# The per-layer products of a hybrid decoder layer, moved from the first expert block into the first attention tile

## The chip, the cores and the metric

The kernel runs on one core of a Trainium2 chip, in float32. The metric is the device time of one execution in microseconds (us). TensorE (PE) multiplies, VectorE (DVE) and ScalarE (ACT) work on elements, GpSimd (POOL) does small operations and indexed transfers, and SyncE (SP) issues most of the DMA transfers. Each engine takes its own instructions strictly in order; they meet only at semaphores.

## The reference

One layer: attention with two groups of heads, a mixture of experts, and a gated embedding per layer (PLE), at SEQ = 512 and D = 1024.

```python
a = rms_norm(h, g_mix); proj = a @ w_in
h = h + concat([o_moba, o_gla]) @ w_out          # two groups of heads
f = rms_norm(h, g_ffn)
h = h + moe_ffn(f, w_router, b_router, w1, b1, w2, b2)   # top 4 of 32 experts
ple = rms_norm(p @ w_ple_proj, g_ple)            # p (512, 256), w_ple_proj (256, 1024)
h = h + sigmoid(h @ w_ple_gate) * ple
return rms_norm(h, g_final)
```

The products `p @ w_ple_proj` depend on inputs alone. They are wanted only at the very end.

## The kernel before

The order of the work on each engine is written out by hand, and semaphores with counts tie the engines together. The stages are: projections (group by group, until 161 us); attention in four tiles of 128 queries, `t` = 0 to 3, each with steps `j` = 0 to 5 on PE (scores, softmax on DVE and ACT, transposed probabilities, values); routing; a first expert block (block 0), written out apart from the rest; a loop over the other blocks of 96 rows; and the tail.

While PE works on attention tile t, it multiplies the mixed heads of tile t - 1 with w_out (`mix_out`, line 1023), DVE adds the halves to H (`add_mix`), and ACT squares the row (`h_square`, line 745). From the square come the mean, the power on POOL, the normed row for the experts (line 1459), and the logits. For the last tile the same chain leads on to the row table `row_of` (line 1650), from which POOL gathers the rows of block 0 (`gather`), PE transposes them, and ACT and DVE take them apart in a high half `XTh` and a low half `XTl`.

Every matrix of the experts is multiplied as a sum of two halves of reduced width. A weight chunk (1 MB, 128x2048) is loaded by SP (`load_chunk`, line 411) into one of six slots, its high half is made by ACT (`split_hi`, line 782) and its low half by DVE (`split_lo`, line 1531), in a ring HL of four. `w_lo` counts the low halves done. Block 0 takes the chunks in the order 0, 1, 2, 3, 8, 6, 7, 9, 10, 11. Slots 0 to 3 lie in the large buffer W, slots 4 and 5 (`W45`) where `wst[:, 0]` lies, the staging buffer of w_in and of the first half of w_out. The bias b1 goes to `b1raw`, ACT copies its high half to BB ahead of `XTh` (line 796), and DVE makes its low half (line 1665) ahead of `XTl`.

The PLE work stood in block 0. SP loaded w_ple_proj and p into `wst[:, 0]` when w_out was nearly done with (lines 461 and 462). PE transposed p (line 1151, to `pT`) and made 16 products of 128x128 by 128x512 in float32 (`ple_tile`, line 1180), each of which the trace shows as two pieces. ACT squared each tile of results straight from PSUM (line 804), POOL took the power, and ACT scaled it (line 808) into `pleo`, in `wst[:, 1]`.

## Time and profile before

| | |
|---|---|
| median of 3 runs | 1537.45 us (1536.6 to 1537.8) |
| the profiled execution | 1536.28 us |
| its span, first to last instruction | 1534.1 us |
| mean granted TensorE clock | 0.988 of 2.4 GHz |
| start of attention, entry into the loop of experts | 162 us, 361.6 us |
| PE busy, DVE busy, ACT busy | 97%, 83%, 65% |

All places in the trace are given in us from the span's start. A row of the timeline reads: start, length, engine, line, operation, output and inputs, count, and in brackets how long the engine had been idle and who released it. Pieces that are merged into one row follow each other without a gap worth mention. A row of the chain reads start, length, what. A busy share says nothing of which engine is late; the chain and the brackets do.

### The profile page before, as it was taken

To read this page: it belongs to the slowest core of one execution; us is meant where nothing else is said; L and a number is where in the kernel's file an instruction comes from. 1 tells how busy PE (TensorE), PEld (TensorE's weight loads), DVE (VectorE), ACT (ScalarE), POOL (GpSimd) and SP (SyncE) were. 2 spreads that over 40 slices of the span, in tenths; PEclk is the share of its full clock that TensorE was granted. 3 is DMA by queue.
4 is the path that set the end of the run, shared out by engine and by line. 5 is a ranking of instruction groups with operands and counts; after the bars stand their busy time and mean duration, and the time that the engine had idled before them with its cause. 6 is when DMAs were issued, how large, how long until landed. Compare 5 with 4: busy or idle time off the path is not lost.

```text
span 1534.1 us, 20725 instructions
## 1 busy us (share of the span) xinstructions
PE 1494.5 (97%) x7115; PEld 1041.7 (68%) x7115; DVE 1280.0 (83%) x1109; ACT 1004.8 (65%) x919; POOL 198.5 (13%) x148
## 2 busy tenths in 40 slices
PE   7999899999999999999999999999999999999997
PEld 5878555566666666676666666666666666666666
DVE  5322356689999999999999999999999999999974
ACT  5432333457777777777777777777777777777642
POOL 6000000020211111111111121111111111111000
PEclk9999799989999999999999999999999999999999
DMA  5215400459999999999999999999999999999921
GB/s 171 98 67 192 178 15 14 157 188 355 374 393 370 372 376 381 375 379 381 380 382 376 377 377 370 375 372 387 373 384 376 382 381 375 380 376 367 380 100 55
DMA packets 126384, 466.58 MB, mean 304 GB/s; under 512 B 7955, under 2 KB 8518, under 8 KB 126358
## 3 DMA queue, kind: packets, MB, share of 16 engines
q1 hardware_dynamic: 118432, 438.73, 75.5%
q0 software_dynamic: 7312, 25.40, 6.8%
q10 hardware_dynamic: 614, 2.11, 0.3%
q8 instruction: 16, 0.26, 0.1%
q14 instruction: 10, 0.08, 0.0%
HBM read 446.67 MB, written 19.53 MB: 304 GB/s over the span
## 4 chain that ended last, share of the span: by engine, by line
PE 94%; DVE 2%; issue 2%; ACT 2%; DMA 0%; POOL 0%; DVEq 0%; POOLq 0%; ACTq 0%
PE ps L1217 46%; PE ps L1249 23%; PE ps L1004 9%; PE ps L1023 3%; PE ps L1347 2%; PE ps L1205 1%; PE ps L1256 1%; PE ps L1232 1%; PE ps L1180 1%; PE ps L1082 1%; PE ps L1070 1%; PE ps L1098 1%; PE ps L1108 1%; PE ps L1042 0%; DMA b_all<-in_b_router_dram 0%
## 5 line engine op out<-in xcount | busy, mean ns | idle before, releaser
L1531 DVE TENSOR_TENSOR HL<-W,HL 128x2048 fp32r<-128x2048 f32 x384 | 881.7, 2321 | 43.2 <-ACT HL L782 40.5
L782 ACT ACTIVATE HL<-W 128x2048 fp32r<-128x2048 f32 x382 | 731.9, 1917 | 174.7 <-PE ps L1217 100.6
L1217 PE MATMUL ps<-HL,XTh 128*96 128x512 f32 x2048 | 563.5, 397 | 0.5 <-DVE XTl L1527 0.5
L1217 PEld LDWEIGHTS ps<-HL,XTh 128*96 128x96 f32 x2048 | 323.2, 162 | 132.9 <-issue 1.9
L1217 PE MATMUL ps<-HL,XTl 128*96 128x512 f32 x1024 | 319.7, 393 | 0.0
L1249 PE MATMUL ps<-HL,HIDTh 128*96 128x512 f32 x1024 | 280.9, 396 | 1.7 <-DVE HIDTl L1559 1.3
L1249 PEld LDWEIGHTS ps<-HL,HIDTh 128*96 128x96 f32 x1024 | 162.7, 161 | 81.8 <-issue 13.2
L1217 PEld LDWEIGHTS ps<-HL,XTl 128*96 128x96 f32 x1024 | 165.2, 161 | 70.5
L600 POOL DMA_INDIRECT y_sums<-actT,row_of x31 | 60.8, 1962 | 949.4 <-ACT actT L841 949.4
L1249 PE MATMUL ps<-HL,HIDTl 128*96 128x512 f32 x512 | 159.6, 393 | 0.0
L1249 PEld LDWEIGHTS ps<-HL,HIDTl 128*96 128x96 f32 x512 | 82.7, 161 | 35.3
L1392 DVE TENSOR_TENSOR PWl<-wst,PWh 128x1024 fp32r<-128x1024 f32 x24 | 29.0, 1223 | 69.0 <-ACT PWh L667 68.1
L583 POOL DMA_INDIRECT XG<-f_rows,row_of x33 | 83.6, 2534 | 17.3 <-DVE row_of L1650 8.2
L812 ACT ACTIVATE HIDTh<-ps 128x384 fp32r<-128x384 f32 x64 | 31.5, 492 | 61.3 <-PE ps L1256 61.1
L1023 PE MATMUL ps<-wst,actT 128*128 128x512 f32 x128 | 58.9, 603 | 0.0
L673 ACT ACTIVATE W<-ps 128x512 f32<-128x512 f32 x20 | 11.9, 594 | 65.2 <-PE ps L1004 65.2
L729 ACT ACTIVATE M<-M,nmax 128x128 f32<-128x128 f32 (+3 forms) x32 | 18.0, 561 | 46.3 <-DVE nmax L1500 46.2
L1555 DVE TENSOR_TENSOR HIDr<-T,SIG 96x512 f32<-96x512 f32 x64 | 44.0, 688 | 5.0
L1497 DVE SCALAR_TENSOR_TENSOR M<-dist,ps 128x128 f32<-128x128 f32 (+3 forms) x32 | 15.4, 483 | 36.7 <-PE ps L1070 27.9
L817 ACT ACTIVATE SIG<-T 96x512 f32<-96x512 f32 x64 | 40.0, 624 | 9.3 <-DVE T L1543 8.3
L823 ACT ACTIVATE XTh<-ps 128x768 fp32r<-128x768 f32 x32 | 26.0, 813 | 28.3 <-PE ps L1217 26.0
L1543 DVE TENSOR_SCALAR T<-ps 96x512 f32<-96x512 f32 x64 | 43.5, 679 | 1.0 <-PE ps L1217 1.0
(270 smaller groups left out, 1378.8 us busy)
## 6 DMA issues: line engine op xcount, KB each, us to landing
W<-in_w_dram SPq DMA_DIRECT2D x384, 1024.0 KB, 8.3
wst<-in_w_in_dram SPq DMA_DIRECT2D x6, 2048.0 KB, 8.6
H<-in_x_dram SPq DMA_DIRECT2D x8, 512.0 KB, 5.0
wst<-in_w_out_dram SPq DMA_DIRECT2D x2, 2048.0 KB, 10.9
W<-in_w_ple_gate_dram SPq DMA_DIRECT2D x4, 1024.0 KB, 7.7
y_sums<-M SPq DMA_DIRECT2D x1, 2688.0 KB, 15.5
f_rows<-M ACTq DMA_DIRECT2D x4, 512.0 KB, 2.6
out_dram<-TL SPq DMA_DIRECT2D x4, 512.0 KB, 2.6
```

Of the source, the lines that this page charges most:

```text
L583: pool.indirect_dma_start(XG[:], None, f_rows, bass.IndirectOffsetOnAxis(ap=row_of[:, b:b + 1].bitcast(U32), axis=0)).then_inc(xg_in, 16)
L600: pool.indirect_dma_start(y_sums, bass.IndirectOffsetOnAxis(ap=rows.bitcast(U32), axis=0), YR, None, compute_op=ALU.add).then_inc(y_added, 16)
L782: act.activation(HL[:, k % HRING, 0], w_slot(k), ACT.Copy).then_inc(w_hi, 1)
L812: act.activation(HIDTh[:, 4 * h:4 * h + 4], ps[:, 2 * h, 0:4 * CAP].rearrange("p (f j) -> p f j", f=4), ACT.Copy).then_inc(hth_out, 1)
L817: act.activation(SIG[:], T1[:], ACT.Sigmoid, scale=ALPHA).then_inc(sig_done, 1)
L1004: last = pe.matmul(ps[:, g % 4], l, r, start=(c == 0 and m == 0), stop=(c == NC - 1 and m == 2))
L1023: last = pe.matmul(ps[:, bank], actT[:, c, t * P:(t + 1) * P], wst[:, n, c], start=(c == first_c), stop=(c == last_c))
L1217: last = pe.matmul(ps[0:CAP, 2 * h + n], xt[:, c], HL[:, s, part, cc * 1024 + n * 512:cc * 1024 + (n + 1) * 512], start=(h == 0 and c == 0 ...
L1249: last = pe.matmul(ps[0:CAP, 4 + n], ht[:, f], HL[:, s, part, ff * 1024 + n * 512:ff * 1024 + (n + 1) * 512], start=(f == 0 and ht is HIDT ...
L1531: dve.tensor_tensor(HL[:, k % HRING, 1], w_slot(k if ready is None else k - 4), HL[:, k % HRING, 0].bitcast(F32), ALU.subtract).then_inc(w ...
L1543: dve.tensor_scalar(t1, ps[0:CAP, 2 * h:2 * h + 2, 0:512:2], LIMIT, None, ALU.min).then_inc(glu_min, 1)
L1555: dve.tensor_tensor(HIDr[:, h * 512:(h + 1) * 512], T2[:], SIG[:], ALU.mult).then_inc(hid_ready, 1)
```

## The change

The PLE products go into attention tile 0. PE transposes p at step 0 and makes two halves of a tile at each of the steps 1 to 4 (`ple_half`), into PSUM banks 3 and 2, and ACT copies them out (`ple_out`). ACT squares them in tile 1 and scales them in tile 2, one tile of results at each of the steps 0 to 3; one operation of DVE and one of POOL, at the start of tile 2, serve all four. The results stay in the first 4096 columns of W. Weight slots 0 and 1, which were there, move to `W01`, which lies where `wst[:, 1]` lies, the second half of w_out. Their first chunks are therefore loaded once that half has been used, for which PE now multiplies the last tile's second half first. On DVE the low half of chunk 0 is made later.

```diff
-        wpp = wst[:, 0, 0:4, :]...
-        prow = wst[:, 0, 4:6, :]...
-        pT = wst[:, 0, 6:8, :]
-        pleo = wst[:, 1, :, :]...
+        wpp = in_w(18432, 2, D)
+        prow = in_w(20480, NT, PLE)
+        pT = in_w(21504, 2, SEQ)
+        pleo = in_w(0, NT, D)
...
-            return W[:, s * 2048:(s + 1) * 2048] if s < 4 else W45[:, s - 4]
+            return W01[:, s] if s < 2 else W[:, s * 2048:(s + 1) * 2048] if s < 4 else W45[:, s - 4]
...
                 if n == 0:
                     sp.wait_ge(p_lo, 24)
+                    sp.wait_ge(st_ready, 14)
+                    sp.wait_ge(kt_ready, 2)
+                    sp.dma_start(wpp, w_ple_proj[0]...).then_inc(ple_ld, 16)
+                    sp.dma_start(prow, p[0, 0]...).then_inc(ple_ld, 16)
...
-            for k in range(2):
-                load_chunk(sp, 0, k, 0)
             sp.wait_ge(s_done, NT * MH)
             for k in range(2, 4):
                 load_chunk(sp, 0, k, 0)
             sp.wait_ge(wo_done, 2 * NT - 1)
-            sp.dma_start(wpp, w_ple_proj[0]...).then_inc(ple_ld, 16)
-            sp.dma_start(prow, p[0, 0]...).then_inc(ple_ld, 16)
+            for k in range(2):
+                load_chunk(sp, 0, k, 0)
             sp.wait_ge(w_lo, 1)
             load_chunk(sp, 0, 6, 0)
...
-            sp.wait_ge(pp_done, NT)
             for k in range(10, NK):
                 load_chunk(sp, 0, k, 0)
...
             for t in range(NT):
+                if t == 2:
+                    pool.wait_ge(pp_ms, 1)
+                    pool.tensor_tensor(rstd[:, 0:NT], ss[:, 0:NT], mhalf[:, 0:NT], ALU.pow).then_inc(pp_rs, 1)
                 go_rstd(t)
...
+            def ple_out(j):
+                if j == 0:
+                    for c in range(2):
+                        act.wait_ge(pt2_done, c + 1)
+                        act.activation(pT[:, c], ps[:, 3 - c], ACT.Copy).then_inc(pt2_out, 1)
+                else:
+                    for i in (2 * j - 2, 2 * j - 1):
+                        act.wait_ge(pp_done, i + 1)
+                        act.activation(pleo[:, i // 2, (i % 2) * 512:(i % 2 + 1) * 512], ps[:, 3 - i % 2], ACT.Copy).then_inc(pp_out, 1)
...
+                    if t == 0:
+                        ple_out(j)
                     for i in (2 * j - 2, 2 * j - 1):
                         if j >= 1:
                             pt_copy(t * MH + i)
+                    if t == 1 and j < NT:
+                        ple_square(j)
+                    if t == 2 and j < NT:
+                        ple_scale(j)
...
             split_x(0)
-            ple_square(0)
             choose_bias(0)
-            ple_scale(0)
-            ple_square(1)
             split_hi(0, 8)
-            ple_scale(1)
-            ple_square(2)
-            ple_scale(2)
-            ple_square(3)
-            ple_scale(3)
             split_hi(0, 6)
...
-                first_c, last_c = (4, 3) if last_tile and n == 0 else (0, NC - 1)
-                bank = 5 - n if last_tile else 3
+                first_c, last_c = (4, 3) if last_tile else (0, NC - 1)
+                bank = 4 + n if last_tile else 3
...
+                    if t == 0 and j == 0:
+                        turn_ple()
+                    elif t == 0 and j <= MH // 2:
+                        ple_half(2 * j - 2)
+                        ple_half(2 * j - 1)
...
                     if j == MH // 2:
                         pe.wait_ge(on_ready, t + 1)
+                        if t == 0:
+                            pe.wait_ge(pp_out, 2 * NT)
...
-            split_lo(0, 0)
-            half_turned(T3, 0, 2 * T3 + 1)
-            add_mix(T3, 1, 4)
-            half_turned(T3, 1, 2 * T3 + 2)
+            half_turned(T3, 1, 2 * T3 + 1)
+            add_mix(T3, 0, 4, 2 * T3 + 2)
+            half_turned(T3, 0, 2 * T3 + 2)
...
             dve.wait_ge(x_asked, 1)
+            split_lo(0, 0)
             split_lo(0, 1)
             dve.wait_ge(bb_hi, 1)
```

SP's queue from the attention tiles to the first expert block, before. `in_w` is an expert's weight chunk, `in_b` the bias; the waits are in brackets, by semaphore.

```order
L411 DMA W<-in_w_dram 128x2x1024 x2
L411 DMA W<-in_w_dram 128x2x1024 [waits s_done]
L411 DMA W<-in_w_dram 128x2x1024
L461 DMA wst<-in_w_ple_proj_dram 128x2x1024 [waits wo_done]
L462 DMA wst<-in_p_dram 128x4x256
L411 DMA W<-in_w_dram 128x2x1024 [waits w_lo]
L467 DMA actT<-in_b_dram 32x512 [waits lg_done]
```

And now:

```order
L413 DMA W<-in_w_dram 128x2x1024 [waits s_done]
L413 DMA W<-in_w_dram 128x2x1024
L413 DMA W<-in_w_dram 128x2x1024 [waits wo_done]
L413 DMA W<-in_w_dram 128x2x1024
L413 DMA W<-in_w_dram 128x2x1024 [waits w_lo]
L471 DMA actT<-in_b_dram 32x512 [waits lg_done]
```

Chunks 0 and 1 stood ahead of the wait for the scores and now stand behind the wait for the last tile's w_out products. The wait for `w_lo` stands where it stood, ahead of chunk 6 and the bias.

DVE behind the last tile's ranks, before. The row with HL is the low half of chunk 0, `ps` is PSUM, `ss` the mean of the FFN norm:

```order
L1610 TENSOR_TENSOR M<-it_j,Js 128x1152 [waits dve_step]
L1531 TENSOR_TENSOR HL<-W,HL 128x2048 [waits w_hi]
L1463 COPY actT<-ps 128x4x128 [waits ft_done]
L1449 TENSOR_TENSOR H<-H,ps 128x512 [waits wo_done]
L1463 COPY actT<-ps 128x4x128 [waits ft_done]
L1365 TENSOR_SCALAR ss<-ss 128x1 [waits h_ss]
```

And DVE now, from the row table on, where the low half of chunk 0 has gone:

```order
L1649 SCALAR_TENSOR_TENSOR row_of<-ps,none 96x32 [waits dve_step]
L1654 TENSOR_REDUCE s<-ex 128x4 [waits e_out]
L1655 RECIPROCAL s<-s 128x4 [waits dve_step]
L1656 TENSOR_TENSOR gate<-ex,s 128x16 [waits dve_step]
L1657 TENSOR_SCALAR extra<-cnt 128x32 [waits dve_step]
L1659 SCALAR_TENSOR_TENSOR extra<-cnt,extra 128x32 [waits dve_step] x4
L1660 SCALAR_TENSOR_TENSOR xend<-ones,extra 128x32 [waits dve_step]
L1531 TENSOR_TENSOR HL<-W,HL 128x2048 [waits w_hi,x_asked,dve_step]
L1531 TENSOR_TENSOR HL<-W,HL 128x2048 [waits w_hi]
L1665 TENSOR_TENSOR BB<-actT,BB 128x512 [waits bb_hi]
```

The low half of chunk 0 has moved past both halves of the last tile, the logits, the row table and the request for the gathered rows, and stands directly ahead of that of chunk 1.

ACT at the end of attention, now as before but for the line numbers; the four rows with HL are the high halves of chunks 0 to 3, the row with H the square of the last tile:

```order
L806 ACTIVATE HL<-W 128x2048 [waits w_slot_in0]
L806 ACTIVATE HL<-W 128x2048 [waits w_slot_in1]
L806 ACTIVATE HL<-W 128x2048 [waits w_slot_in2]
L806 ACTIVATE HL<-W 128x2048 [waits w_slot_in3]
L763 ACTIVATE M,ss<-H 128x1024 [waits f_stored,h_ready]
```

The order has not moved there, but what the first two wait for has: their chunks come later.

## Rows read from the trace of the kernel before

**Rows 1.** The page, part 4: shares of the chain that ended last, by line.

```profile
PE ps L1217 46%; PE ps L1249 23%; PE ps L1004 9%; PE ps L1023 3%; PE ps L1347 2%; PE ps L1205 1%; PE ps L1256 1%; PE ps L1232 1%; PE ps L1180 1%; PE ps L1082 1%; PE ps L1070 1%; PE ps L1098 1%; PE ps L1108 1%; PE ps L1042 0%; DMA b_all<-in_b_router_dram 0%
```

**Rows 2.** Windows: stretch, length, then busy us of PE, PEld, DVE, ACT, POOL.

```profile
309.40:352.90 43.50, 42.81 (x190) 26.69 (x190) 38.75 (x69) 23.95 (x29) 10.07 (x12) 0.93 0.63 203
```

**Rows 3.** Timeline of DVE, end of attention to the loop.

```profile
295.20 2.28 DVE L1531 TENSOR_TENSOR HL<-W,HL 128x2048 fp32r<-128x2048 f32 x1
...
309.97 0.19 DVE L1650 SCALAR_TENSOR_TENSOR row_of<-ps,none 96x32 int32<-96x32 f32 x1
312.03 0.17 DVE L1655 TENSOR_REDUCE s<-ex 128x4 f32<-128x16 f32 x1 [1.87 <-ACT ex L792]
...
316.24 0.68 DVE L1665 TENSOR_TENSOR BB<-actT,BB 128x512 fp32r<-128x512 f32 x1
...
318.03 4.48 DVE L1531 TENSOR_TENSOR HL<-W,HL 128x2048 fp32r<-128x2048 f32 x2
...
352.46 2.29 DVE L1531 TENSOR_TENSOR HL<-W,HL 128x2048 fp32r<-128x2048 f32 x1 [0.88 <-ACT HL L782]
```

**Rows 4.** The chain that ended last, in order of time.

```profile
183.92 1.94 PE ps L1058 x8
...
213.54 1.13 PE ps L1058 x8
...
311.94 3.67 PE ps L1180 x4
...
330.62 3.43 PE ps L1180 x8
...
360.72 0.88 DVE XTl L1527
361.60 0.04 issue
361.64 5.81 PE ps L1217 x24
```

**Rows 5.** Groups by line, 309.4 to 352.9: busy us, mean ns; idle before.

```profile
L1180 PE MATMUL ps<-wst 128*128 128x512 f32 x32 | 16.3, 656 | 0.7 <-ACT wst L790 0.7
...
L1151 PE MATMUL ps<-ident,wst 128*128 128x128 f32 x8 | 1.9, 425 | 0.0
```

**Rows 6.** Groups by line of PE, 161 to 186 (attention tile 0).

```profile
L1098 PE MATMUL ps<-ident,M 128*128 128x128 f32 x8 | 2.8, 447 | 4.5 <-DVE M L1483 4.5
```

**Rows 7.** Windows in tile 0; the number behind POOL's is the granted clock.

```profile
176.00:178.00 2.00, 1.04 (x6) 0.79 (x6) 1.82 (x7) 0.99 (x4) 1.06 (x1) 0.50 1.03 409
```

**Rows 8.** Timeline of ACT, end of attention to the first expert block.

```profile
282.94 7.30 ACT L782 ACTIVATE HL<-W 128x2048 fp32r<-128x2048 f32 x4
300.13 1.06 ACT L745 ACTIVATE M<-H 128x1024 f32<-128x1024 f32 x1 [9.89 <-DVE H L1449]
...
313.42 0.61 ACT L796 ACTIVATE BB<-actT 128x512 fp32r<-128x512 f32 x1
316.31 0.81 ACT L823 ACTIVATE XTh<-ps 128x768 fp32r<-128x768 f32 x1 [2.28 <-PE ps L1205]
```

**Rows 9.** Timeline of SP: when it issued.

```profile
291.65 0.37 SPq L461 DMA_DIRECT2D wst<-in_w_ple_proj_dram  x1
...
297.52 0.37 SPq L411 DMA_DIRECT2D W<-in_w_dram  x1
303.59 2.11 SPq L467 DMA_DIRECT2D actT<-in_b_dram  x4
```

**Rows 10.** Line 411, pairs of chunks: first at 273, then at 334.

```profile
DMA to landing us min/median/max: 7.0/8.0/9.0
...
DMA to landing us min/median/max: 4.8/5.9/6.9
```

**Rows 11.** DMA issues: count, KB each, us from issue to landing.

```profile
W<-in_w_dram SPq DMA_DIRECT2D x1, 1024.0 KB, 5.6
...
actT<-in_b_dram SPq DMA_DIRECT2D x4, 64.0 KB, 2.8
...
actT<-in_g_ple_dram SPq DMA_DIRECT2D x1, 512.0 KB, 7.8
```

More of the change, by code:

```diff
@@ L181, in hybrid_layer @@
         oh_tok = M[:, 4640:5152].rearrange("p (a e) -> p a e", e=NE)
[L184 removed]
+        BB, _, HIDr, HIDTh, HIDTl, T1, T2, SIG, XG, XTh, XTl, W45, W01, sel = scope(
             ("BB", [P, D], F32R), ("skip7", [P, 2048], F32),
@@ L446, in _ @@
                     sp.wait_ge(p_lo, 24)
+                    sp.wait_ge(st_ready, 14)
+                    sp.wait_ge(kt_ready, 2)
+                    sp.dma_start(wpp, w_ple_proj[0].rearrange("(c p) n -> p c n", p=P)).then_inc(ple_ld, 16)
+                    sp.dma_start(prow, p[0, 0].rearrange("(t p) n -> p t n", p=P)).then_inc(ple_ld, 16)
                 else:
@@ L589, in _ @@
             pool.tensor_tensor(asked[:], tok[0:1, 0:1], tok[0:1, 0:1], ALU.add).then_inc(x_asked, 1)
-            for t in range(NT):
-                pool.wait_ge(pp_ss, t + 1)
-                link(pool.tensor_scalar(ss[:, 5:6], ss[:, 7:8], 1.0 / D, EPS, ALU.mult, ALU.add))
-                pool.tensor_tensor(rstd[:, 5:6], ss[:, 5:6], mhalf[:, 0:1], ALU.pow).then_inc(pp_rs, 1)
-                pool.wait_ge(pp_rs, t + 1)
-                if t == 1:
-                    gather(1)
+            gather(1)
             def add_rows(rows):
@@ L787, in _ @@
             store_f(NT - 1)
-            for c in range(2):
-                act.wait_ge(pt2_done, c + 1)
-                act.activation(pT[:, c], ps[:, 4 + c], ACT.Copy).then_inc(pt2_out, 1)
             act.wait_ge(e_in, 1)
@@ L1047, in _, with turn_ple, ple_half @@
             pe.wait_ge(consts, 17)
+            def turn_ple():
+                pe.wait_ge(ple_ld, 32)
+                for c in range(2):
+                    for t in range(NT):
+                        last = pe.transpose(ps[:, 3 - c, t * P:(t + 1) * P], prow[:, t, c * P:(c + 1) * P], ident[:])
+                    last.then_inc(pt2_done, 1)
+            def ple_half(i):
+                if i == 0:
+                    pe.wait_ge(pt2_out, 2)
+                elif i >= 2:
+                    pe.wait_ge(pp_out, i - 1)
+                t, n = i // 2, i % 2
+                for c in range(2):
+                    last = pe.matmul(ps[:, 3 - i % 2], pT[:, c, t * P:(t + 1) * P], wpp[:, c, n * 512:(n + 1) * 512],
+                                     start=(c == 0), stop=(c == 1))
+                last.then_inc(pp_done, 1)
             MIX_STEPS = [range(0, 5), range(5, 8), range(8, 13), range(13, 16)] + 2 * [range(0)]
@@ L1135, in _ @@
             pe.matmul(ps[:, 7, 0:T3 * NE], before[:], Mk[:, 0:T3], start=False, stop=True).then_inc(rank_done, 1)
-            for c in range(NC):
-                if c == 5:
+            for c in (4, 5, 6, 7, 0, 1, 2, 3):
+                if c == 1:
                     pe.wait_ge(lg_out, T3)
-                    turn_h(T3, 0)
-                mix_out(T3, 1, c)
+                    turn_h(T3, 1)
+                mix_out(T3, 0, c)
             def slot_tokens(a0, a1):
@@ L1147, in slot_tokens @@
                     last.then_inc(tok_done, 1)
-            def turn_ple(c):
-                for t in range(NT):
-                    last = pe.transpose(ps[:, 4 + c, t * P:(t + 1) * P], prow[:, t, c * P:(c + 1) * P], ident[:])
-                last.then_inc(pt2_done, 1)
             pe.wait_ge(oh_ready, 1)
@@ L1169, in _ @@
             slot_tokens(A3, A)
-            pe.wait_ge(ple_ld, 32)
-            for c in range(2):
-                turn_ple(c)
-            def ple_tile(t, parts=(0, 1)):
-                a = 2 + 2 * (t % 2)
-                if t >= 2:
-                    pe.wait_ge(pp_out, t - 1)
-                for n in parts:
-                    for c in range(2):
-                        last = pe.matmul(ps[:, a + n], pT[:, c, t * P:(t + 1) * P], wpp[:, c, n * 512:(n + 1) * 512],
-                                         start=(c == 0), stop=(c == 1))
-                if parts[-1] == 1:
-                    last.then_inc(pp_done, 1)
-            pe.wait_ge(pt2_out, 2)
-            pe.wait_ge(lg_out, NT)
-            ple_tile(0, (0,))
             def gate_tables():
                 pe.wait_ge(gate_oh, 1)
-                pe.wait_ge(pp_out, NT)
                 for a in range(A):
@@ L1442, in _, with add_mix @@
                 dve.tensor_tensor(rg[:, t], rg[:, t], tmpG[:, 0], ALU.mult).then_inc(rg_ready, 1)
-            def add_mix(t, n, bank=3):
-                dve.wait_ge(wo_done, 2 * t + n + 1)
+            def add_mix(t, n, bank=3, count=None):
+                dve.wait_ge(wo_done, 2 * t + n + 1 if count is None else count)
                 if t == 0:
@@ L1490, in _ @@
                     dve.wait_ge(go_done, t)
+                if t == 2:
+                    dve.wait_ge(pp_ss, NT)
+                    dve.tensor_scalar(ss[:, 0:NT], ss[:, 0:NT], 1.0 / D, EPS, ALU.mult, ALU.add).then_inc(pp_ms, 1)
                 dve.copy_predicated(AT, chunk_ok[:].rearrange("p h q -> p (h q)"), ps[:, 1]).then_inc(a_out, 1)
```

46 lines of the change are left out of this document (17 added, 29 removed).

## The prediction

> **What bounds the kernel now.** I read the page first [rows 1]: 94% of the chain that ended last is TensorE's (PE). Most of that is the expert loop (lines 1217 and 1249), which the change does not alter. The change touches two places ahead of it: attention tile 0 (162.6 to 183.9 us) and the stretch from the end of attention to the loop. There the busy share misleads. Between 309.4 and 352.9 PE is busy for 42.8 of 43.5 us, but VectorE (DVE) for 38.8 as well [rows 2], and most of the rest lies ahead of 312.03, where its gap of 1.87 us for the exponential ends; after that I find one larger gap, 0.88 us near the end [rows 3]. The chain enters the loop through DVE: the low half of the gathered rows, XTl, ends at 361.6, and PE's first product of the loop starts at 361.64 [rows 4]. So DVE is the one that is late at the loop's door, and PE's work in that stretch is covered. The reader is to see that two engines are full there, and that only the later one sets the end.
>
> **What leaves the head of the experts.** 32 pieces of L1180, 16.3 us, and 8 transposes at L1151, 1.9 us, of PE [rows 5]: 18.2 us. ScalarE (ACT) loses two copies, four squares and four scalings, GpSimd (POOL) eight small operations. If DVE sets the end, PE's 18.2 us bring nothing, and what ACT loses brings DVE one thing: it no longer waits 1.87 us for the exponential [rows 3], which stood behind the pT copies on ACT.
>
> **What tile 0 gets.** On PE 8 transposes and 16 products. At full clock 8 pieces of L1180 take 3.43 us, at half clock 4 take 3.67 [rows 4]; so 32 pieces are 13.7 us at full clock and 29.4 at half, and with the transposes (1.9 us measured, mostly at half) the addition is 15 to 31 us. Tile 0 took 21.3 us, from 162.60, where PE could start, to 183.92 [rows 4]. 4.5 us of it PE waited for scaled probabilities [rows 6], and the clock stood at 0.50 in the stretch shown [rows 7], that is 1.2 GHz, after such waits. With products between the waits PE is dense from about 167 on. I take full clock. The other 16.8 us, small products and short waits, then shrink by less than half (the eight products that open tile 1 took 1.94 us, those that open tile 2 at full clock 1.13 [rows 4], a ratio of 0.6): 10.1. The new work adds 15.5, and I leave 1.6 us for waits for ACT's copies of the projections: 27.2 in all, +5.9. The opening products of tile 1 run at full clock too, which gives 0.8 back: **+5.1**. Should the clock stay low for the first 4 to 6 us, add 2 to 3. Those copies (ten of 128x512, 0.6 us each, the price of the bias copy [rows 8]) fit beside PE otherwise.
>
> The Trainium skill, "TensorE: Matmul & The Clock Gate", Part 1, says that the throttled state is the default and that activity releases it; the 0.50 in the sparse tile agrees with it. By that page the whole addition is paid near full clock; if it failed here, the low-clock rival below would be the case.
>
> **ACT in tiles 1 and 2.** Each of the four squares (1.06 us and a short read, as the square of H at 300.13 [rows 8]) and scalings lies in slack, except the last of each tile. It stands just ahead of the square of H, which releases the FFN rows, their copies, and PE's next tile. That is **+1.2** for tile 1. Tile 2 has more cover, and DVE gets one tiny operation: **+1.0**. Bounds: 0 and 1.3 each.
>
> **The weight chunks 0 and 1.** They used to be loaded during attention, since the first 4096 columns of W were free; now the results live there and the chunks go to where the second half of w_out lies. They are issued where w_ple_proj was, at 291.65 [rows 9]. Pairs of 1 MB landed 4.8 and 6.9 us after their issue in one place (334) and 7.0 and 9.0 in another (273) [rows 10], so chunk 0 lands at 296.5 to 298.7, chunk 1 (issued 0.4 later) at 299.0 to 301.1. ACT's order is not changed: four splits of 1.83 us, then the square of H of the last tile. Before, the four ended at 290.2, and the square began at 300.13, as soon as H was ready [rows 8]. Now the second split begins at about 299.5, three take 5.5, and the square begins at 305.0: **+4.9** (4.4 to 6.5). Queued behind it are the last FFN rows, the logits, and the row table at 309.97 to 310.16 [rows 3]. PE waits 5 us more in between, so its short rank products may be slow: +0.5. The row table stands at 315.6.
>
> **The low half of chunk 0 moves on DVE** from 295.20, where DVE had time, to behind the row table [rows 3]: 2.2 us more on the full engine. From 312.03 to 318.03 before lie a split (2.2), the low half of the bias (0.6), XTl with a short wait (0.88 and 0.2) and so 2.1 us of small operations [rows 3, 4]. Now these start at 315.6 and end at 317.7, and chunk 0's low half ends at 319.9.
>
> **The wait that this lengthens.** SyncE (SP) waits for exactly that (w_lo at least 1) before it loads chunk 6, and the bias b1 is queued behind it. Before, chunk 6 went at 297.5 and b1 at 303.59, when the logits were wanted [rows 9]. Now chunk 6 goes at 319.9 and the four pieces of b1 at 320.4 to 321.9. They landed in 2.8 us when alone; a 1 MB chunk needs 5.6; and g_ple, half a megabyte behind two chunks, needed 7.8 [rows 11]. The low bound is 321.9 + 2.8 = 324.7, the high one 328; I take chunk 6's landing, 325.5, and half a microsecond: **326.0**, since g_ple's case is the nearest. Behind that wait on ACT stand the bias copy (0.61) and the high half of XT (0.81) [rows 8], and DVE waits for both. XT's high half is there at 327.4, XTl at 328.3. In the old trace the next split began at 318.03 [rows 3]: **+10.3** (8.5 to 13).
>
> The Trainium skill, "DMA: Bandwidth & Descriptors", HWDGE ordering, says that descriptors are consumed in ring order on each engine, which would put b1 behind chunk 6 (326.0); the 2.8 us of b1 alone would give 324.7. No row shows this very pair.
>
> From there DVE has the same work as before. Its late waits for ACT (0.88 and about 0.1 us, ACT being held by PE's use of chunks 6 and 7) should go, as PE is no longer late [rows 3]: **-1.0**. Chunks 10 and 11 are issued earlier with respect to their use, so they hide. PE's 18.2 us buy just this.
>
> **Sum.** 5.1 + 1.2 + 1.0 + 10.3 - 1.0 = +16.6 us. The profiled execution took 1536.3 us, so 1552.9; the median is 1.2 above it: **1554 us**.
>
> **Rivals.** (1) PE is the bound ahead of the loop, as its 42.8 of 43.5 us suggest, and loads and bias hide: -18.2 + 7.3 = -10.9, 1526.6 us. Against it stands the chain's entry through XTl [rows 4] and DVE's own count. It decides if DVE's work shrinks or is waited for less than I read. Chance 0.07. (2) The bias does not hold: b1 lands before DVE wants it. DVE then starts its small operations 3.6 us late, and has 2.2 us more: +5.8 - 1.0 + 7.3 = +12.1, 1549.6. It needs b1 at 322, before the low bound. 0.08. (3) The clock stays at 1.2 GHz in all of tile 0: 16.8 + 31 against 21.3 is +26.5 instead of +5.1, in all +38, 1575. For it: the tile ran so before; against it: PE will be nearly without gaps. 0.05. (4) The change does not do what it says in effect: the copies and loads hide so well that what attention pays is about what the head gains, within 3 us of 1537.5. 0.03. (5) The forecast, with its bounds: 0.77.
>
> **Numbers.** The low ends together (tile 0 4.5, tiles 1 and 2 0.5, head 8.5 - 1.5) give +12, 1549.5; the high ends (8.5, 2.3, 13) +23.8, 1561. Rival 2 lies at the lower end. With a margin for several small terms the range is 1545 to 1563. Faster or slower is told apart here from 0.2%, 3 us: faster 0.07, same 0.03, slower 0.90.
>
> **What would show it.** Right: square of H of the last tile near 305 + 7.4 = 312 behind the splits; b1's issue on SP just after the low half of chunk 0, at about 328; DVE waiting about 5 us ahead of the low half of the bias; PE with gaps ahead of chunk 8; the loop entered at about 378 rather than 361.6, with nothing changed behind. Wrong: XTl within 3 us of its old place, PE without gaps in the first block, or tile 0 longer by 10 us and more.

## The result, and the profile after

The changed kernel took **1557.34 us** (median, 1555.5 to 1558.1), the kernel before 1537.62 us beside it: a ratio of 1.0126, with a 95% interval of 1.0108 to 1.0143. The forecast was slower, 1554 us, with a range of 1545 to 1563. The direction and the mechanism held; the amount was 19.7 us where 16.5 was forecast, and the missing 3 us lie in a few terms that are named below.

The profiled execution of after took 1555.53 us with a span of 1553.7, against 1536.28 and 1534.1 before. First where the extra time is. The shortest way is to cut both timelines at the same operations: the first product of attention tile 0, the last half of H, the square of H, the row table, the start of XTl of block 0 and of block 1 (the door of the loop). Each number is a difference of two starts.

| stretch | before | after | difference |
|---|---|---|---|
| start of attention, at | 162.60 | 162.59 | 0.0 |
| tile 0 | 21.25 | 27.93 | +6.7 |
| tile 1 | 29.69 | 29.88 | +0.2 |
| tile 2 | 33.68 | 35.57 | +1.9 |
| tile 3, to the last half of H | 52.18 | 52.18 | 0.0 |
| last half of H to the square of H | 0.73 | 7.02 | +6.3 |
| square of H to the row table | 9.84 | 9.56 | -0.3 |
| row table to XTl | 7.18 | 13.27 | +6.1 |
| XTl of block 0 to XTl of block 1 | 43.49 | 42.24 | -1.2 |
| from there to the end | 1173.5 | 1173.5 | 0.0 |

The sum is +19.6, the difference of the spans. The last row is worth a look: the loop and all that follows take the same time to within 0.1 us in every kernel of this study (1173.4 to 1173.5), so whatever a kernel gains or loses is settled by the time that it enters the loop. The stretch from XTl to XTl, which the argument needs most, is read from these rows of DVE, first before, then after:

```profile
317.15 0.96 DVE L1527 TENSOR_TENSOR XTl<-ps,XTh 128x768 fp32r<-128x768 f32 x1 [0.23 <-ACT XTh L823]
...
360.64 0.94 DVE L1527 TENSOR_TENSOR XTl<-ps,XTh 128x768 fp32r<-128x768 f32 x1
```

```profile
380.24 0.94 DVE L1527 TENSOR_TENSOR XTl<-ps,XTh 128x768 fp32r<-128x768 f32 x1
```

(The first XTl of after, at 338.00, stands further down.)

**Tile 0.** The timeline of PE in after (start, us, engine, line, operation, tiles, count, idle ahead of it in brackets) shows the new products, now line 1065, eight records for two half tiles:

```profile
164.10 1.09 PE L1054 MATMUL ps<-ident,W 128*128 128x128 f32 x8
...
167.13 3.70 PE L1065 MATMUL ps<-W 128*128 128x512 f32 x8 [1.32 <-ACT W L743]
...
174.93 3.70 PE L1065 MATMUL ps<-W 128*128 128x512 f32 x8
...
184.74 0.44 PE L1102 MATMUL ps<-M,W 128*64 128x128 f32 x4 [0.81 <-ACT M L737]
...
190.52 1.16 PE L1078 MATMUL ps<-W 128*128 128x128 f32 x8
```

Four groups of 3.70 and 1.09 for the transposes are 15.9 us, and the waits in brackets are short: PE stood idle for 3.2 us of the whole tile, against 6.0 before. The products that open tile 1 took 1.16 us at 190.52, where [rows 4] have 1.94. The granted clock says why; in the windows below it is the number behind POOL's (a mean of stretches at 2.4 and at 1.2 GHz), first for before, then for after, 162 to 184:

```profile
162.00:184.00 22.00, 15.44 (x77) 9.56 (x77) 9.85 (x34) 9.02 (x30) 1.06 (x1) 0.57 0.83 311
```

```profile
162.00:184.00 22.00, 19.52 (x94) 10.56 (x94) 9.96 (x34) 10.90 (x32) 1.06 (x1) 1.00 0.59 215
```

**The end of attention.** ACT's timeline, to be held against [rows 8], and SP's against [rows 9]:

```profile
307.28 1.91 ACT L806 ACTIVATE HL<-W 128x2048 fp32r<-128x2048 f32 x1 [15.48 <-DMA W<-in_w_dram]
309.76 5.51 ACT L806 ACTIVATE HL<-W 128x2048 fp32r<-128x2048 f32 x3 [0.57 <-DMA W<-in_w_dram]
315.17 1.04 ACT L763 ACTIVATE M<-H 128x1024 f32<-128x1024 f32 x1
...
336.64 0.63 ACT L817 ACTIVATE BB<-actT 128x512 fp32r<-128x512 f32 x1 [12.07 <-DMA actT<-in_b_dram]
```

```profile
300.39 29.12 SPq L413 DMA_DIRECT2D W<-in_w_dram  x3
329.56 1.99 SPq L471 DMA_DIRECT2D actT<-in_b_dram  x4
```

The square of H has no wait of its own (no bracket): it stands at 315.17 because the four splits do, and the second of them waited for chunk 1, which landed 8.9 us after its issue (chunk 0 6.9). The three issues that share SP's first line are chunks 0 and 1 at 300.4 and 300.8, and chunk 6, which goes 29 us later, just ahead of b1. DVE's timeline has the two waits that this makes; [rows 3] have neither:

```profile
316.34 0.15 DVE L1362 TENSOR_SCALAR ss<-ss 128x1 f32<-128x1 f32 x1 [6.06 <-ACT M L763]
...
326.83 4.50 DVE L1531 TENSOR_TENSOR HL<-W,HL 128x2048 fp32r<-128x2048 f32 x2
337.30 0.69 DVE L1665 TENSOR_TENSOR BB<-actT,BB 128x512 fp32r<-128x512 f32 x1 [5.97 <-ACT BB L817]
338.00 0.96 DVE L1527 TENSOR_TENSOR XTl<-ps,XTh 128x768 fp32r<-128x768 f32 x1
```

And the chain of after, followed from the first split on DVE to the next, is the argument in a few rows: the split, SP's queue with chunk 6 (L413) and b1 (L471), the landing, ACT's copy.

```profile
326.83 2.30 DVE HL L1531
329.15 0.37 SPq L413
329.52 0.04 issue
329.56 0.46 SPq L471
...
331.13 5.48 DMA actT<-in_b_dram
336.61 0.02 issue
336.64 0.64 ACT BB L817
```

**The first expert block.** PE now has four gaps between XTl of block 0 and that of block 1, 1.2 to 1.6 us each, and DVE's name is in each bracket. DVE itself has no gap from XTl to XTl. Two of the four:

```profile
355.34 1.17 PE L1219 MATMUL ps<-HL,XTh 128*96 128x512 f32 x4 [1.54 <-DVE HL L1531]
...
369.42 1.18 PE L1219 MATMUL ps<-HL,XTh 128*96 128x512 f32 x4 [1.48 <-DVE HL L1531]
```

### The profile page after: what moved, and what is told of

Its sections match the earlier page's. It is cut to its first block, busy times and chain, and to the rows that moved or that the text cites. A ratio compares the mean times of both kernels' runs of the same rounds, so it can differ in the third digit from the quotient of the medians.

```text
span 1553.7 us, 20722 instructions
## 1 busy us (share of the span) xinstructions
PE 1490.8 (96%) x7115; PEld 1039.6 (67%) x7115; DVE 1280.1 (82%) x1110; ACT 1008.4 (65%) x927; POOL 192.4 (12%) x141
## 4 chain that ended last, share of the span: by engine, by line
PE 74%; DVE 3%; issue 1%; ACT 1%; DMA 0%; SPq 0%; DVEq 0%; POOLq 0%; POOL 0%; ACTq 0%
PE ps L1219 44%; PE ps L1251 22%; PE ps L1344 2%; PE ps L1258 1%; PE ps L1207 1%; DVE HL L1531 1%; PE ps L1234 1%; PE ps L1311 0%; DMA actT<-in_b_dram 0%; ACT HL L901 0%; PE ps L1324 0%; PE ps L1172 0%; ACT HL L801 0%; DVE XTl L1527 0%; DVE M L1691 0%
## 5 line engine op out<-in xcount | busy, mean ns | idle before, releaser
L1219 PE MATMUL ps<-HL,XTh 128*96 128x512 f32 x2048 | 564.1, 397 | 12.4 <-DVE XTl L1527 8.2
L1497 DVE SCALAR_TENSOR_TENSOR M<-dist,ps 128x128 f32<-128x128 f32 (+3 forms) x32 | 15.5, 484 | 37.9 <-PE ps L1090 29.4
L1550 DVE SCALAR_TENSOR_TENSOR T<-T 96x512 f32<-96x512 f32 x64 | 43.6, 681 | 0.2
## 6 DMA issues: line engine op xcount, KB each, us to landing
y_sums<-M SPq DMA_DIRECT2D x1, 2688.0 KB, 15.5
```

The costliest lines, as they stand in the source:

```text
L1219: last = pe.matmul(ps[0:CAP, 2 * h + n], xt[:, c], HL[:, s, part, cc * 1024 + n * 512:cc * 1024 + (n + 1) * 512], start=(h == 0 and c == 0 ...
L1550: dve.scalar_tensor_tensor(out=T2[:], in0=T2[:], scalar=1.0, in1=T1[:], op0=ALU.add, op1=ALU.mult).then_inc(moe_step, 1)
```

## Experiments

Two theories are on trial. Mine: DVE is the engine that sets the end ahead of the loop, so the 18.2 us taken off PE buy about 1 us, and after pays for tile 0, for ACT's splits in front of the square, and for b1 behind chunk 6 behind chunk 0's low half. The rival: PE was the bound there, and its 18.2 us are given back somewhere. Attention, below, is the time from its start to the last half of H; the other stretches are those of the table, each from the one profile of its kernel. The kernel before took between 1537.4 and 1538.6 us (medians) beside the various experiments, so two medians of different experiments are compared to about 1 us only.

### The bias put ahead of chunk 6

```diff
+            sp.wait_ge(lg_done, NT)
+            for r in range(4):
+                sp.dma_start(b1raw[r * NE:(r + 1) * NE, :], b1[0, :, r * 512:(r + 1) * 512]).then_inc(bias_in, 16)
+            sp.dma_start(b2s, b2[0]).then_inc(b2_in, 16)
             sp.wait_ge(w_lo, 1)
             load_chunk(sp, 0, 6, 0)
-            sp.wait_ge(lg_done, NT)
...
```

> The changed kernel, with one thing moved on SP: the four pieces of b1 and b2 are issued as soon as the logits are done, ahead of the wait for the first low half and of chunk 6. Theory (the bias holds ACT and with it XTl): b1 has landed before the row table is written, DVE goes from the low half of chunk 1 straight to that of the bias, and XTl is held only by the gathered rows, at about 332 instead of 338.0: 6 us less than the changed kernel, 1551.3 us. Rival (something else, DVE's own work or the gather, would hold XTl as long): within 1.5 us of the changed kernel's 1557.3.

Measured: 1550.14 us, ratio 1.0083 (1.0066 to 1.0100), 7.2 us less than after; the two profiles are 7.1 apart. Row table to XTl fell from 13.27 to 7.32, and DVE goes from the splits to the bias and XTl with no bracket between:

```profile
325.72 4.49 DVE L1531 TENSOR_TENSOR HL<-W,HL 128x2048 fp32r<-128x2048 f32 x2
330.13 0.68 DVE L1665 TENSOR_TENSOR BB<-actT,BB 128x512 fp32r<-128x512 f32 x1
330.94 0.96 DVE L1527 TENSOR_TENSOR XTl<-ps,XTh 128x768 fp32r<-128x768 f32 x1
```

The last half of H to the square stayed at 7.13 and XTl to XTl at 42.23. So 5.95 us of after are this wait. Most of the rest between the profiles is attention, 143.99 against 145.56, where the two kernels have the same code (see the clock, below). b1 landed 2.0 us after its issue here, alone, and 5.5 after it behind chunk 6.

### The last square put ahead of the splits

```diff
-            for k in range(4):
-                split_hi(0, k)
             h_square(NT - 1)
+            split_hi(0, 0)
             store_f(NT - 1)
+            for k in range(1, 4):
+                split_hi(0, k)
```

> The changed kernel, with one thing moved on ACT: the square of H of the last tile goes ahead of the four splits of chunks 0 to 3 (the store of the FFN rows behind the first split). Theory (the last tile's square stood behind chunks that landed late): the square is at 308.9 instead of 315.2, the row table at 318.7 instead of 324.8, and everything behind it 6.1 us earlier: 1551.2 us. The wait of DVE for the bias stays at about 6 us. Rival (the 6 us are slack since the bias is what is late, and its load hangs on chunk 0): under 2 us less, above 1555.

Measured: 1551.09 us, ratio 1.0087 (1.0070 to 1.0104). Last half of H to the square is 0.72 again, as before the change, and last half of H to the row table 10.58, against 16.58 in after. The bias wait is still there, and DVE's is somewhat longer (6.71 against 5.97), so that row table to XTl is 13.99:

```profile
314.67 1.06 ACT L763 ACTIVATE M<-H 128x1024 f32<-128x1024 f32 x1 [17.09 <-DVE H L1447]
...
337.16 0.63 ACT L818 ACTIVATE BB<-actT 128x512 fp32r<-128x512 f32 x1 [11.54 <-DMA actT<-in_b_dram]
```

```profile
337.82 0.69 DVE L1666 TENSOR_TENSOR BB<-actT,BB 128x512 fp32r<-128x512 f32 x1 [6.71 <-ACT BB L818]
```

So 6.3 us are the order of ACT's queue. From the last half of H to the loop the kernel gained 5.3 (66.81 against 72.09), as the longer wait took some of it back. Its profile hides this: attention took 148.91 us there, 3.3 more than in after, with the same code up to that point (the clock, below).

### Both

> Both moves of the two runs before it. Theory (two terms in one chain, which add up): 12 us less than the changed kernel, 1545.3 us; what is left over the kernel before is what attention pays (8.75 us) less about 1. Rival (the two waits overlap): 6 to 8 us less, 1549 to 1551.

Measured: 1543.89 us, ratio 1.0045 (1.0031 to 1.0059). From the last half of H to the loop 60.58 us, against 72.09 in after and 61.24 before. The two moves alone had gained 5.9 and 5.3 there, and together they gain 11.5, so the two faults add up. The head of the experts is then 0.7 us better than before, and all that is left of the loss is attention, 144.00 against 136.80: +7.2. (The prediction had 7.3 for attention in sum; this run's own expectation had 8.75.)

### Chunk 0's low half put back among the H rows of DVE

In after it was behind the row table. Here it stands behind the second half of H (in before it stood just ahead of that).

```diff
             half_turned(T3, 0, 2 * T3 + 2)
+            split_lo(0, 0)
             ffn_mean(T3)
...
             dve.wait_ge(x_asked, 1)
-            split_lo(0, 0)
             split_lo(0, 1)
```

> The changed kernel, with the low half of chunk 0 on DVE put back ahead of the row table, into the 6 us in which DVE waits for the square of H; SP and ACT as in the change. Theory: the first low half is done at about 312.5 instead of 329.1, so chunk 6 and b1 are issued then, no one waits for the bias, and DVE has 2.2 us less behind the row table; XTl is then held by the gathered rows at about 331.5: 6.4 us less, 1550.9 us. Rival (only the 2.2 us of work count): 1555.

Measured: 1550.31 us, ratio 1.0090 (1.0064 to 1.0117). The split fits into DVE's wait for the square (3.86 left of 6.06) and frees chunk 6 early:

```profile
310.78 2.28 DVE L1531 TENSOR_TENSOR HL<-W,HL 128x2048 fp32r<-128x2048 f32 x1
316.92 0.15 DVE L1362 TENSOR_SCALAR ss<-ss 128x1 f32<-128x1 f32 x1 [3.86 <-ACT M L763]
...
332.51 0.96 DVE L1527 TENSOR_TENSOR XTl<-ps,XTh 128x768 fp32r<-128x768 f32 x1 [2.21 <-ACT XTh L832]
```

Row table to XTl is 7.20, the same as with the bias first. The 2.2 us that the split takes behind the row table are thus worth nothing by themselves: without it DVE waits them out for the high half of XT, which waits for the gathered rows. The prediction had called them work on the full engine, and rival 2 charged them as such. What they cost was b1's place in SP's queue, not DVE's time.

### Without the squares and scalings

The per-layer rows are left unnormalized: the four squares, the mean, the power and the four scalings are gone.

> The changed kernel without the four squares and four scalings of the PLE rows on ACT in tiles 1 and 2, and without the two small operations of DVE and POOL that go with them: the norm of the PLE rows is left out. Theory (the last square and the last scaling stand ahead of the square of H): tile 2 starts 1.1 us earlier and tile 3 another 1.9 us earlier, with the clock at 2.4 GHz at the start of tile 2: 2.9 us less, 1554.4 us. Rival (they lie in slack and the growth of tiles 1 and 2 has another cause): within 0.7 us of 1557.3.

Measured: 1553.45 us, ratio 1.0097 (1.0070 to 1.0123); attention 142.65. Against 144.0 in the kernels that have them and whose clock stood at 1.00 in tile 2 that is 1.35 us for all of them, where I had 1.2 + 1.0: 1.0 in tile 1 (28.84 against 29.88) and 0.3 in tile 2. Against after, whose clock fell there, it is 2.9, as this run's expectation had it.

### After without any per-layer work

The transposes, the product, its copies, squares and scalings are left out, and the per-layer rows are zero.

> The changed kernel without any PLE work on PE, ACT and DVE: no transposes, products, copies, norm (the PLE rows are zeros written by POOL); loads and memory places as in the change. Theory: attention is back at its old length, 8.75 us less, and the head of the experts is as in the change: 1548.6 us, still 11 us above the kernel before. Rival (tile 0's products fill gaps and the loss is all in the head): within 3 us of 1557.

Measured: 1549.20 us, ratio 1.0069 (1.0043 to 1.0095). Attention 138.44, 1.6 us above what it was before; that lies in tile 1, in which POOL now writes the zeros for 3.7 us, and whether this is the cause was not tested. H to the loop stays at 72.38, against 61.24 before. So the layout and the order alone, with no product anywhere, cost over 11 us at the head, and the work in attention the rest.

### Before without any per-layer work

This is the test of the rival: PE's 18.2 us and ACT's work gone, nothing added anywhere. The per-layer rows are not computed.

> The kernel before, with the PLE work in the first expert block left out and put nowhere (no transposes, products, copies, squares, scalings; its loads stay): 18.2 us of PE work less. Theory (DVE is as late as PE there): PE falls idle, XTl of block 0 stays where the gathered rows allow it, and only the two late waits of DVE, 1.0 us, go: 1536.5 us. Rival (PE is the bound ahead of the loop): up to 18 us less, 1520 to 1530.

Measured: 1536.94 us against 1538.62, ratio 0.9990 (0.9978 to 1.0002). XTl to XTl 42.24, where before has 43.49: 1.25 us.

```profile
318.39 0.96 DVE L1498 TENSOR_TENSOR XTl<-ps,XTh 128x768 fp32r<-128x768 f32 x1 [2.05 <-ACT XTh L813]
...
360.63 0.94 DVE L1498 TENSOR_TENSOR XTl<-ps,XTh 128x768 fp32r<-128x768 f32 x1
```

PE's 18.2 us and ACT's share together are worth 1.25 in this stretch. In this profile even that was lost again ahead of it: the square to the row table took 11.06 us, against 9.84, with PE's mean clock at 0.59 there instead of 0.75. The medians are 1.7 us apart, and the interval takes in no difference. The first rival of the prediction would have had some 18, and it falls here by itself, without any of the change's side effects.

### Which engine, then

If DVE alone set this stretch, taking work off it should help in the kernel before. In the first of two runs the exponential goes ahead of the pT copies on ACT, and one low half ahead of XTl on DVE, where DVE otherwise waits:

```diff
+            act.wait_ge(e_in, 1)
+            act.activation(ex4[:], ex4[:], ACT.Exp).then_inc(e_out, 1)
             for c in range(2):
                 act.wait_ge(pt2_done, c + 1)
                 act.activation(pT[:, c], ps[:, 4 + c], ACT.Copy).then_inc(pt2_out, 1)
-            act.wait_ge(e_in, 1)
-            act.activation(ex4[:], ex4[:], ACT.Exp).then_inc(e_out, 1)
...
-            rest_x(0)
             split_lo(0, 2)
+            rest_x(0)
             split_lo(0, 3)
```

> The kernel before with two moves that give DVE 2 us in block 0: the exponential ahead of the pT copies on ACT, and the low half of chunk 2 ahead of XTl. Theory (both engines are full there, so that relief of DVE alone brings nothing, as PE is then the late one): within 0.5 us of the kernel before; DVE's gap near 352 grows from 0.9 to about 3 us. Rival (DVE alone is the bound): 2 us less, 1535.5.

Measured: 1538.97 us, ratio 1.0000 (0.9985 to 1.0015). XTl to XTl 43.27. The 2.2 us taken off DVE came back as two gaps in which it waits for ACT:

```profile
345.52 2.29 DVE L1531 TENSOR_TENSOR HL<-W,HL 128x2048 fp32r<-128x2048 f32 x1 [1.73 <-ACT HL L782]
```

```profile
356.83 2.29 DVE L1531 TENSOR_TENSOR HL<-W,HL 128x2048 fp32r<-128x2048 f32 x1 [1.16 <-ACT HL L782]
```

Ahead of the first, ACT's split stood behind the last per-layer scaling, which waited for POOL's power and through it for PE's last product; ahead of the second, behind HIDTh, which waited for PE. PE itself ran without a gap from the gathered rows to the loop.

The second run is the kernel before without per-layer work (as above) with the same low half ahead of XTl, so both sides are relieved. One wait of DVE, that for the request of the gathered rows, is left out as well.

> The kernel before without the PLE work in block 0, as in the run e8 that left it out, and with the low half of chunk 2 ahead of XTl on DVE, into its wait for the gathered rows. Each of the two alone moved the entry into the loop by 1.25 us at most. Theory (both engines are full and either one holds the loop): together they give DVE's 2.2 us as well, so XTl of block 0 to XTl of block 1 takes 40.0 us instead of 42.24 and the row table to XTl 7.3: 3.4 us less than the kernel before, about 1534. Rival (a third thing, the loads or the gather of block 1, holds the entry): 42 us from XTl to XTl, 1536.5.

Measured: 1533.61 us against 1537.57, ratio 0.9971 (0.9960 to 0.9983). XTl to XTl 40.05: now the 2.2 us do come off.

```profile
319.71 0.96 DVE L1498 TENSOR_TENSOR XTl<-ps,XTh 128x768 fp32r<-128x768 f32 x1
...
359.76 0.94 DVE L1498 TENSOR_TENSOR XTl<-ps,XTh 128x768 fp32r<-128x768 f32 x1
```

The window from its row table to the loop, 312.5 to 360: PE 36.8 us busy, DVE 46.0 of 47.5.

```profile
312.50:360.00 47.50, 36.83 (x184) 25.97 (x184) 46.03 (x75) 19.51 (x18) 3.68 (x4) 0.87 0.72 239
```

So there are two bounds of nearly equal height: 42.24 is DVE's, about 43.3 is that of PE with the per-layer product. Relieving either alone gains 1.25 us or 0.2 (43.49 to 42.24 or to 43.27); both together gain 3.4. One thing stays open here. The runs without per-layer work take the product off PE and the copies, squares and scalings off ACT at once, and in the first run above one of DVE's two gaps passes through ACT's scaling. How much of the 43.3 is the product and how much ACT's order behind it was not separated.

### The last square and scaling moved back on ACT

On top of both repairs, the last per-layer square and scaling stand behind ACT's last copy of their attention tile instead of ahead of the square of H.

```diff
-                    if t == 1 and j < NT:
+                    if t == 1 and j < NT - 1:
                         ple_square(j)
-                    if t == 2 and j < NT:
+                    if t == 2 and j < NT - 1:
                         ple_scale(j)
...
+                if t == 1:
+                    ple_square(NT - 1)
+                if t == 2:
+                    ple_scale(NT - 1)
                 if t >= 1:
                     store_f(t - 1)
```

> The changed kernel with both moves of the run e3 (bias first, square of H first), and with the last square and the last scaling of the PLE rows moved behind ACT's last copy of their tile, off the path to the next tile. Theory: attention takes 142.7 us instead of 144.0 at full clock, the rest is as in e3: 1542.5 us, the best of the moved layout and still 5 us above the kernel before, since tile 0 pays 5.8 and the head gives back less than 1. Rival (ACT was slack there, the 1.35 us have another cause): 1543.9 as e3.

Measured: 1540.45 us, ratio 1.0024 (1.0015 to 1.0033). Attention 142.28 where both repairs alone have 144.00. This saves 1.7 us, 0.4 more than taking all of them away (142.65), which is not explained; so the position of the last one is about the whole price of the squares and scalings, as I had read. H to the loop is 60.10. What is left is tile 0. The median fell by 3.4 us, more than the 1.7 and the 0.5 at the head that the two profiles show; the part on the clock below has a likely reason.

### Half of the product in tile 0

In after, only the first four of the eight half tiles are computed; the rows of the other two tiles are zero.

```diff
-                    elif t == 0 and j <= MH // 2:
+                    elif t == 0 and j <= MH // 4:
                         ple_half(2 * j - 2)
                         ple_half(2 * j - 1)
```

> The changed kernel with only the first four of the eight PLE halves: the products and copies of PLE tiles 2 and 3 are left out of steps 3 and 4 of attention tile 0 (their rows are zeros), all else as in the change. It measures what the second half of the dense work costs in tile 0. Theory (tile 0 is bound by PE once the products are in it and the clock stays at 2.4 GHz; the first products fill old gaps): 8 products, 6.9 us, and a gap of about 1 us less, while old waits of up to 2 us come back: tile 0 is 5.5 to 6.5 us shorter than in the change, about as long as in the kernel before, so the first half was nearly free: 1551.5 us. Rival (the second half is as free as the first, the cost lies in the fixed parts, transposes and first copies): 2 to 3 us shorter, 1554.5.

Measured: 1551.59 us, ratio 1.0086 (1.0069 to 1.0103). Tile 0 took 20.78 us, against 27.93 with the whole product and 21.25 before, with none (20.94 to 21.01 in four other profiles with none). Half of the product is free; the second half costs 7.1 us, its 7.4 us of PE nearly in full, and more than the 5.5 to 6.5 that I expected. The transposes and the first four half tiles are some 8.5 us of PE. Of these, 3.0 went into gaps (PE idle 2.98 us of the tile, 5.96 before), and the rest into what full clock gives back: PE's clock in 162 to 184 is 1.00 with 18.63 us busy. The median fell by less than tile 0 did (5.8), as row table to XTl took 14.39 us here, 1.1 more than in after; why b1 came later was not looked into.

```profile
162.00:184.00 22.00, 18.63 (x97) 10.92 (x96) 8.82 (x29) 10.12 (x28) 2.99 (x3) 1.00 0.61 216
```

### A version with the product split over both places

Four half tiles go into tile 0, where they are free, and four into PE's wait for the gathered rows, where the kernel before had one; both repairs are in, and ACT's split of chunk 3 moves behind the last half tile. Nothing is left out.

```diff
+            pe.wait_ge(lg_out, NT)
+            for i in (4, 5, 6):
+                late_half(i)
             pe.wait_ge(row_ready, 2)
             turn_x(0)
+            late_half(7)
             first_expert()
```

> The product is split over the two places: the first four of its eight half tiles in attention tile 0 as in e10_half, their squares and scalings (two each) in tiles 1 and 2; the other four half tiles on TensorE behind the slot tokens, where it waits for the gathered rows (three ahead of the transposes of XG, one behind them), with their squares and scalings on ScalarE as the kernel before had them; b1 loads ahead of chunk 6 and the last square ahead of the splits (as e3_both). Nothing of the computation is left out. Theory (half of the product is free in tile 0, and what is left fits into the wait of row to XTl): attention as in e10_half, 136.85 us, less up to 0.7 for two squares and two scalings fewer; last half of H to the end of the square 0.7; row to XTl 7.2; XTl to XTl of block 1 42.3; last half of H to the loop 60.1 to 60.6 where the kernel before has 61.24. Sum of attention and this stretch 196.3 to 197.5 against 198.04 before, so 1535.9 to 1537.1 against 1537.6. Rival (the late half tiles delay the transposes of XG or the split that waits for their weights): row to XTl 9 or more, or XTl to XTl 44 or more, time 1539 or more.

Measured: 1537.50 us against 1538.06, ratio 0.9994 (0.9984 to 1.0003): it can't be told from the kernel before. Inside it both theories met. Attention took 135.14 us, 1.7 less than before and 1.0 to 1.7 less than I expected: tile 0 took 20.78 us, tile 1 0.85 shorter than before since its opening products find full clock, tile 2 0.36 shorter. XTl to XTl is 42.32. But row table to XTl is 9.12, as the rival had it:

```profile
307.97 8.23 PE L1327 MATMUL ps<-W 128*128 128x512 f32 x12
316.04 0.82 PE L1234 MATMUL ps<-ident,XG 96*128 96x96 f32 x8
```

```profile
308.00:316.00 8.00, 8.00 (x13) 3.37 (x14) 7.13 (x14) 2.09 (x5) 1.54 (x3) 0.64 0.38 105
```

Three half tiles took 8.2 us, 2.7 each, where they took 1.85 each in tile 0: the mean clock was 0.64. In the kernel with both repairs the gathered rows were there 4.8 us after the row table (318.55 to 323.31); here their transposes began 7.4 after it (308.62 to 316.04). With two half tiles ahead of the rows instead of three, PE would have been done at about 313.5 by the same rows, when the rows come. That was not run.

## Why the prediction was right, and where it was short

**Who sets the end ahead of the loop: right, but not whole.** The 18.2 us of PE bought 1.25 us (forecast 1.0). The kernel before without per-layer work shows the same 1.25. What I had called one full engine and one covered is two bounds about 1 us apart; the prediction needed only that DVE was among them. The gap of 1.87 us for the exponential went as forecast, but gave nothing, as XTl is held by the gathered rows: row table to XTl was 7.0 to 7.3 in before and in each kernel whose bias came in time, but for the version with the product split, where PE was late for those rows (9.12).

**Tile 0: mechanism right, 0.8 short.** Full clock, the product and the shrinking of the rest came as worked out. 27.93 us against 27.2; less the 0.8 of the opening products, +5.9 where I wrote +5.1. The transposes and products took 15.9 and not 15.5. In it two errors nearly cancel: the products took 14.8 us where I had 13.7, and the transposes 1.1 where I had 1.8. The 3.43 us for eight pieces came from a row of the chain, which begins where the chain enters the group; the timeline of PE has the same group at 330.46 with 3.59 us. All the rest of the tile, its waits included, took 12.0 us where I had 10.1 and 1.6. The Trainium skill, "TensorE: Matmul & The Clock Gate", Part 1, has activity release the throttle; the tile at 0.57 without the product and at 1.00 with half or all of it agrees.

**Tiles 1 and 2: 2.2 forecast, 2.9 measured.** With a clock of 1.00 at the door of tile 2 they cost 1.3, 1.0 in tile 1 and 0.3 in tile 2, and attention 7.2 in all. That this meets the 7.3 of the forecast is partly luck: tile 0 was 0.8 dearer than forecast, and these two 0.9 cheaper. The other 1.6 us of after are a clock of 0.86 there, and that did not come in each run:

```profile
218.00:230.00 12.00, 10.41 (x46) 6.23 (x42) 5.85 (x13) 3.09 (x7) 1.02 (x1) 0.86 0.11 46
```

```profile
218.00:230.00 12.00, 10.40 (x55) 6.10 (x56) 6.07 (x14) 3.45 (x7) 1.11 (x2) 1.00 0.11 46
```

The first is after, the second the run with the bias first, whose code is the same up to there and whose PE was as busy. In the run with the square first the mean clock was 0.72 and attention took 148.9 us. So a single profile of these kernels can hold 1.6 or 4.9 us that do not belong to the edit on trial.

They do seem to belong to the change. The last per-layer square stands ahead of the square of H (at 214.73 in after), holds the copies behind it, and so makes PE wait once more and longer ahead of tile 2, here in after:

```profile
217.51 0.66 PE L1102 MATMUL ps<-M,W 128*64 128x128 f32 x8 [0.50 <-ACT M L737]
...
220.40 1.71 PE L1078 MATMUL ps<-W 128*128 128x128 f32 x8 [1.58 <-DVE actT L1460]
```

and here in the run with the last square moved back, where the first of the two waits is gone:

```profile
218.90 1.13 PE L1083 MATMUL ps<-W 128*128 128x128 f32 x8 [1.17 <-DVE actT L1465]
```

Six profiles have the waits of 0.50 and 1.58 us, and in three of them (after, square first, low half back) the clock fell in the two microseconds behind. The other eight wait 1.17 or 1.25 us, and it fell in none. This points to the last square as the cause, by a clock that then falls in some executions only; it would also account for the median of the run that moved it, which gained more than its stretches show. Six profiles do not prove it.

**The last square of H: 4.9 forecast, 6.3 measured.** The term that was off is the landing of chunk 1. I let the second split begin 7.4 us after its issue, between the two pairs of [rows 10] (6.9 and 9.0 for a second chunk). What came was 6.9 us for chunk 0 and 8.9 for chunk 1, the slower pair. That pair (at 273) also lay nearer to the place of issue in the kernel before, by 18 us against 42, and I should have leaned on it. The +0.5 for slow rank products was not there: the stretch behind the square became 0.3 shorter.

**The bias: 4.9 forecast, 6.1 measured, for row table to XTl.** The chain was as described, down to chunk 0's low half ending 4.2 us behind the end of the row table (forecast 4.3). The last issue of b1 began 2.0 us after that low half was done, as forecast (329.13 and 331.13; 319.9 and 321.9 in the forecast). Only the landing was off by much: b1 landed 5.5 us after that issue, where I had 4.1. The Trainium skill, "DMA: Bandwidth & Descriptors", HWDGE ordering, has descriptors consumed in ring order; 2.0 us alone and 5.5 behind a 1 MB chunk agree with that. Rival 2 (the bias does not hold) is what the run with the bias first shows, for 6 us less.

**The rivals.** The first fell by the kernel before without per-layer work, the third by the clock of 1.00, the fourth by the sum. Three terms were off by a microsecond or more, all the same way: two landings, of chunk 1 and of b1, put low between their bounds, and the clock of tile 2, which the sum did not have at all. The signs that I had named came a little late for the same reason: the square of H at 315.2 (312 forecast), b1's issue at 329.6 (328), the door of the loop at 381.2 (378).

**What stays open.** Why the clock falls at the door of tile 2 in some executions and not in others was not settled, nor, beyond what the profiles above suggest, what brings it about. Each kernel has one profile, so how often it falls is not known either. And of the 43.3 us bound, the parts of PE and ACT were not told apart.

## What to carry to other kernels

Work moved off a full engine gains only if that engine is alone in front; count the busy time of the second one, and if both are within a microsecond or two, plan to relieve both or neither. When a load is moved later, go down each in-order queue that waits for it: here two queues (ACT's splits ahead of a square, SP's chunk 6 ahead of a small bias) cost 12.4 us, more than the 8.8 us by which attention grew, and both were repaired by changing the order alone. And fill a sparse, slow-clocked stretch only as far as its gaps and what a faster clock gives back go: the first half of the product was free there, the second cost its full time.

## What the runs showed of the hardware

Adding 8.5 us of products and transposes to attention tile 0 made it no longer (20.78 us, against 20.94 to 21.25 without them), as PE's clock went from 0.57 to 1.00 and 3.0 us of gaps were filled; and where half of the product was there and half of the squares, the next tile gained 0.85 us from it. The same half tile costs 1.85 us at full clock in tile 0, and 2.7 us at 0.64 ahead of the gathered rows, where PE had just done small products with waits. Executions also differ ahead of all that was edited: attention begins between 162.1 and 166.1 us in these profiles, so single spans of two kernels are not to be compared, only stretches cut at the same operations, or medians over rounds.
